# GpSimd computes the pool branch's moving sums ahead of two weight splits, and their consumers move up by two or three steps

## The reference

```python
h = rms_norm(x, g_mix_norm[l])
z = h @ w_in[l]
q_lat, kv_lat, k_rope = z[..., :o1], z[..., o1:o2], z[..., o2:o3]
uv, pin = z[..., o3:o4], z[..., o4:]
a = mla_mixer(...)                       # 4 heads, causal softmax over 512 tokens
gm = sgu_mixer(uv, ...)                  # gate branch
po = pool_mixer(pin, w_pool[l], pool_scale[l])
mix = concatenate([rms_norm(a), rms_norm(gm), rms_norm(po)])
x = x + mix @ w_out[l]

def pool_mixer(p, w_pool, pool_scale):
    for g, win in enumerate((2, 4, 8, 16)):
        # mean over the last `win` tokens, minus the token itself
        outs.append((cs - cs_shift) / count - xg)
    y = einsum('bsgc,gcd->bsgd', m, w_pool)
    return y * pool_scale
```

## Time and profile before

| what | value |
|---|---|
| median of 3 runs | 2698.09 us (2691.52 to 2700.82) |
| profiled execution | 2697.78 us, span 2695.9 us |
| mean granted TensorE clock | 0.985 of full speed |
| PE busy | 2607.8 us, 97% of the span |
| DVE busy | 1173.2 us, 44% |
| ACT busy | 501.1 us, 19% |
| POOL busy | 1626.1 us, 60% |

### The profile page before, as it was taken

One profiled execution on the slowest core, in us unless ns is written; L12 is line 12 of the kernel. 1 busy time (PEld: TensorE's weight loads), 2 busy tenths in 40 slices (PEclk: granted clock), 3 DMA queues, 4 the chain that ended last, 5 costly groups with the idle time before them and its releaser, 6 DMA issues.

```text
span 2695.9 us, 31577 instructions
## 1 busy us (share of the span) xinstructions
PE 2607.8 (97%) x11906; PEld 2142.7 (79%) x11906; DVE 1173.2 (44%) x1678; ACT 501.1 (19%) x849; POOL 1626.1 (60%) x1113
## 2 busy tenths in 40 slices
PE   7889999999899999999999999999999999999997
PEld 6768888888578888887888888888788878888885
DVE  5754443036644440345540513783467155504325
ACT  3342111023421110201200103200310044100022
POOL 5526667664266676666676766676246615767763
PEclk9999999999899999999999999999999999999998
DMA  4102222231022222222232223222112202222221
GB/s 153 63 16 94 97 105 94 93 115 63 16 94 98 104 93 94 94 94 94 102 106 97 93 94 104 93 98 104 48 47 100 103 32 73 94 106 94 94 93 63
DMA packets 36892, 236.71 MB, mean 88 GB/s; under 512 B 4048, under 2 KB 5584, under 8 KB 9168
## 3 DMA queue, kind: packets, MB, share of 16 engines
q1 hardware_dynamic: 33456, 230.78, 24.6%
q10 hardware_dynamic: 3360, 4.85, 0.6%
HBM read 233.51 MB, written 2.10 MB: 87 GB/s over the span
## 4 chain that ended last, share of the span: by engine, by line
PE 93%; DVE 4%; ACT 1%; issue 1%; POOL 0%; DMA 0%; DVEq 0%; SPq 0%; POOLq 0%; ACTq 0%
PE psum L469 29%; PE psum L470 28%; PE psum L471 28%; PE psum L918 2%; PE psum L902 1%; PE psum L680 1%; PE psum L927 1%; PE psum L790 1%; PE psum L806 0%; DVE work L1335 0%; PE psum L499 0%; DMA x_res<-in_x 0%; POOL w_low L411 0%; PE psum L752 0%; DVE stat L1676 0%
## 5 line engine op out<-in xcount | busy, mean ns | idle before, releaser
L411 POOL TENSOR_TENSOR w_low<-w_stage,w_high 128x512 fp32r<-128x512 f32 x864 | 1178.7, 1395 | 18.0
L407 POOL TENSOR_SCALAR w_high<-w_stage 128x2048 fp32r<-128x2048 f32 x216 | 416.3, 1928 | 1014.8 <-PE psum L471 1003.5
L469 PE MATMUL psum<-x_high,w_high 128*128 128x512 f32 x1664 | 654.2, 393 | 17.0 <-DVE x_low L1351 17.0
L470 PE MATMUL psum<-x_low,w_high 128*128 128x512 f32 x1664 | 649.3, 390 | 0.0
L471 PE MATMUL psum<-x_high,w_low 128*128 128x512 f32 x1664 | 649.0, 390 | 0.0
L469 PEld LDWEIGHTS psum<-x_high,w_high 128*128 128x128 f32 x1664 | 313.4, 188 | 85.1 <-issue 17.1
L470 PEld LDWEIGHTS psum<-x_low,w_high 128*128 128x128 f32 x1664 | 313.3, 188 | 67.0 <-issue 2.2
L471 PEld LDWEIGHTS psum<-x_high,w_low 128*128 128x128 f32 x1664 | 313.3, 188 | 65.2
L469 PE MATMUL psum<-mlp_high,w_high 128*128 (+1 forms) x576 | 224.3, 389 | 2.8 <-DVE mlp_low L1468 2.8
L1392 DVE TENSOR_TENSOR psum<-psum,x_res 128x512 f32<-128x512 f32 x56 | 39.2, 700 | 426.8 <-PE psum L471 423.8
L471 PE MATMUL psum<-mlp_high,w_low 128*128 (+1 forms) x576 | 224.2, 389 | 0.0
(11 more groups left out here) (266 smaller groups left out, 3486.2 us busy)
## 6 DMA issues: line engine op xcount, KB each, us to landing
w_stage<-in_wstream SPq DMA_DIRECT2D x216, 1024.0 KB, 4.9
x_res<-in_x SPq DMA_DIRECT2D x2, 1024.0 KB, 11.7
out_x<-attn_out SPq DMA_DIRECT2D x8, 256.0 KB, 2.1
inv_count_sb<-in_inv_count ACTq DMA_DIRECT2D x2, 512.0 KB, 9.0
ple_proj<-in_p ACTq DMA_DIRECT2D x2, 512.0 KB, 3.7
qk<-in_mask ACTq DMA_DIRECT2D x1, 576.0 KB, 3.8
w_spat<-in_spatial ACTq DMA_DIRECT2D x2, 256.0 KB, 5.5
diag_sb<-in_diag ACTq DMA_DIRECT2D x2, 256.0 KB, 9.7
```

The lines of the kernel that those rows point to most:

```text
L407: pool.tensor_scalar(wh[:, s, :], stage[:, s, :], 1.0, 1.0, ALU.mult, ALU.mult).then_inc(high_written, 1)
L411: last = pool.tensor_tensor(wl[:, s, part], stage[:, s, part], wh[:, s, part].bitcast(F32), ALU.subtract)
L469: pe.matmul(out, wa, ra, start=start, stop=False)
L470: pe.matmul(out, wa, rb, start=False, stop=False)
```

## The change

GpSimd does slabs 0 to 5, then the moving sums, then slabs 6, 7 and the rest. Before, it did slabs 0 to 7, then the moving sums, then the rest. On PE `pool_products` moves from step 11 to step 8, and the two `token_sum` jobs from steps 13 and 15 to steps 11 and 13. On ACT `pool_scaled` moves from step 12 to step 10. On DVE `pool_sum` moves from step 14 to step 12. No instruction is added or removed.

```diff
@@ gpsimd
-                    split_run(at, p.slab + 8)
-                    at = p.slab + 8
+                    split_run(at, p.slab + 6)
+                    at = p.slab + 6
                     pool.wait_ge(phase_landed, 16 * (FIRST_LOADS + MIX_LOADS * (p.layer + 1)))
                     windows(p)
@@ tensor
-... 5: gate_products, 11: pool_products,
-    13: lambda: token_sum(p, 2, 2), 15: lambda: token_sum(p, 3, 2)}
+... 5: gate_products, 8: pool_products,
+    11: lambda: token_sum(p, 2, 2), 13: lambda: token_sum(p, 3, 2)}
@@ scalar
-                between = {8: gate_squares, 12: pool_scaled}
+                between = {8: gate_squares, 10: pool_scaled}
@@ vector
-... 9: gate_sum, 14: pool_sum}
+... 9: gate_sum, 12: pool_sum}
```

More of the change, by code:

```diff
@@ L781, in pool_products @@
                         last.then_inc(z_done, 1)
-                between = {1: lambda: input_tile(2), 2: lambda: input_tile(3), 5: gate_products, 11: pool_products,
-                           13: lambda: token_sum(p, 2, 2), 15: lambda: token_sum(p, 3, 2)}
+                between = {1: lambda: input_tile(2), 2: lambda: input_tile(3), 5: gate_products, 8: pool_products,
+                           11: lambda: token_sum(p, 2, 2), 13: lambda: token_sum(p, 3, 2)}
                 def values(h):
@@ L1660, in low_out @@
                         tt(mix_low[k], tile, mix_high[k].bitcast(F32), ALU.subtract).then_inc(split_low, 1)
-                between = {2: lambda: pool_input(0), 3: lambda: pool_input(1), 6: lambda: gate(0), 7: lambda: gate(1), 9: gate_sum, 14: pool_sum}
+                between = {2: lambda: pool_input(0), 3: lambda: pool_input(1), 6: lambda: gate(0), 7: lambda: gate(1), 9: gate_sum, 12: pool_sum}
                 steps = HEADS * TOK
```

## The result

The changed kernel is slower by a little: 2702.25 us median (2698.34 to 2706.14, 20 runs) against 2697.64 us (2691.52 to 2703.84, 20 runs) before, a ratio of 1.0015 with a 95% interval of 1.0009 to 1.0021. That is 4.6 us, within the 0.3% that were forecast as "no change", inside the range of 2691 to 2706, a quarter of a microsecond above the forecast's own range of 2695 to 2702, and not the 0.4 us of the forecast.

The account below looks back on a forecast made before the run. PE and DVE waiting for each other in two 54 us stretches was taken as the bound. Terms of -1.7 + 1.6 + 0.3 gave +0.2 us per phase, +0.4 for two: median 2698.5 us, range 2691 to 2706.

Parts of the forecast that it names:

- the forecast's 141.6: GpSimd, first loop: the splits of slabs 6 and 7 end at about 141.6 us, at no cost to PE.
- What that does to DVE: DVE, steps 6 to 8: instructions wait for GpSimd's splits, making divisions late and costing PE 1.6 us per phase, bounds 0 to 2.9.
- a case at full clock: PE at step 8: at full clock it loses 0.9 us to the division of step 8, ending at 141.6 us.
- one at half clock: PE at `values(1)`: if it runs at half clock as before, step 7's whole 2.3 us of lateness pass through.
- Moving sums earlier: GpSimd: sums start as each tile is ready, from 110.1 us, ending about 126.6; nothing waits for their start.
- The terms behind it: Behind step 8's transposes: pool scaling, token sums and `pool_sum` gain 1.7 us per phase; ACT behind a late DVE costs 0.3.
- Moving the second sum to step 13: PE, step 13: the second token sum costs 0.91 us there, after a 0.6 us wait for `pool_sum`.
- the 0.3 for ACT: ACT, step 10: pool scaling stands behind late exponential and copy, so PE's token sum may wait; 0.3 us per phase.
- the slower rival: Steps 7 to 10: GpSimd's lock beside DVE's critical instructions costs 2.9 us, pool gain lost; 2703 to 2707 us, chance 0.18.
- The move does nothing at step 8: PE, step 8: bank 3 is freed late, so the products merely change place; 1.86 us per phase return, 2702 us; chance 0.05.
- the faster rival: PE, `values(1)` at full clock: DVE's later divisions stay inside PE's own time; some 2693 us in total, chance 0.25.

Follow-up runs that it names:

- e1: The kernel before with only GpSimd's new order (sums, then slabs 6 and 7), jobs of PE, ACT and DVE at their old steps: 2705.86 us, ratio 1.0020 to before.
- e3: The changed kernel with GpSimd waiting, after the sums, for a count reached with step 10's scores before splitting slabs 6 and 7: 2699.78 us, ratio 1.0000 to before.
- e6: The changed kernel with slabs 6 and 7 each split in 8 + 8 short GpSimd instructions instead of 1 + 4: 2695.95 us, ratio 0.9986 to before.
- e2: The changed kernel with slab 6 split ahead of the moving sums and only slab 7 behind them: 2695.42 us, ratio 0.9991 to before.

## Why the prediction was partly right

**What held.** The bound: PE and DVE waiting for each other in two short stretches, and DVE waiting for the end of GpSimd's running instruction. The moving sums started at once. PE did not wait for the late splits themselves. The products went into PE's wait at step 8, and L1685 still ended it. The first token sum stands right behind the scores of step 11. GpSimd's end came at 27.96 us after the scores of step 3, where the forecast's 141.6 is 27.5. Each loop changed by less than 2 us. The total stayed within 0.3%.

**The step that failed: "What that does to DVE".** Its term was 1.6 us a loop, the middle of a case at full clock (0.9) and one at half clock (2.3). It measured 2.94 and 3.02 us, beyond the upper bound of 2.9. Walked from POOL's rows, the division of step 7 was to end 2.3 us late. It ended 135.21 - 111.53 = 23.68 us after the scores of step 3 against 21.08 before, 2.6 us late, and `values(1)`, over its 2.42 us at full clock in both, took 0.34 us more (3.65 against 3.31). The two make 2.94. Of the 1.34 us that the term was short, 0.7 are the choice: nothing in the rows spoke for full clock at `values(1)`. PE had waited for DVE there before, and was to wait again. The case of 2.3 should have been taken, not a mean of two cases, one of which had no row for it.

The walk's 2.3 itself came near by luck, as two errors in it cancel. "Moving sums earlier" was put at no cost, as nothing waits for the start of the sums. But DVE's steps 3 to 5 met them, and the maximum of step 6, where the walk began, was 0.7 us late already (10.23 us after the scores of step 3 against 9.52). From there to the division of step 7 DVE lost 1.9 us, less than the walk's 2.3. In the second loop the parts are others. The division of step 7 ended 3.8 us late (23.46 against 19.70): 1.6 us at the maximum of step 6, half of it the gate products' clock (2.82 us and not 1.97), and 2.2 behind it. `values(1)` gave 0.7 us back, as it took 3.68 us and not 4.39. So its 3.02 is near the first loop's 2.94 by chance. The division of step 8 ended 28.04 us after the scores of step 3, 3.4 us late and not 2.9, but PE reached it another 1.5 us later.

**The terms behind it** came out right in their sum. Forecast -1.7 and +0.3, that is -1.4 us from step 8's transposes to the end of the loop. Measured: 46.62 to 44.67 and 45.72 to 44.64 us, -1.95 and -1.08, a mean of -1.5. That the mean fits is in part luck, as the clock moved both loops: `values(2)` took 4.11 us before and 3.29 after in the first loop, 2.88 and 3.32 in the second. Up to step 11's transposes, where no `values` stands, the gain was 1.2 us in both loops, where 1.3 less the 0.3 for ACT was forecast. ACT's 0.3 did not come: the first token sum starts 0.1 us behind the scores of step 11. Step 11's transposes were to be within 1 us of before and were 1.75 us late, which is the failed term again. Moving the second sum to step 13 was counted at 0.91 us and a wait of 0.6. The wait was 0.96.

**The rivals.** With 2.9 us in the profiles' loops and 4.6 us in the medians, the outcome lies nearer to the slower rival, which began at 5.2 us, than to the forecast of 0.4. That rival had the right mechanism (e1, e3, e6), a place that e1 shows, and a price at step 8 that was right (2.9). It missed that the gain behind step 8 stays, and its sum of 2 x (2.9 - 0.3) doesn't follow from its terms: with the gain gone they give 2 x 2.9 = 5.8 us and more, and no row shows the 0.3. "The move does nothing at step 8" is refuted by the trace. Of the faster rival, no sign: `values(1)` took 3.65 and 3.68 us, not 2.42, and PE ran at 0.81 of its clock in both loops after the change. (The "up to 3" of that rival is 8.21 x (1 - 0.53) = 3.9 by its own row.)

```profile
111.50:165.50 54.00, 39.20 (x171) 24.31 (x169) 41.47 (x91) 26.38 (x62) 26.22 (x20) 0.81 0.11 39
664.60:718.60 54.00, 39.25 (x171) 24.37 (x169) 41.40 (x91) 26.51 (x62) 26.25 (x20) 0.81 0.11 39
```

GpSimd is busy 26.2 us of the 54 where it was 22.4 and 22.7, and DVE's busy time, which holds its waits for GpSimd, grew by 2.4 and 1.8 us. The added split is 7.7 us of GpSimd's time. GpSimd's column grows by less, as the first tile's sums now run largely ahead of the stretch.

**What stays open.** The medians moved by 4.6 us (2.4 to 5.7 by the interval) and the two loops in the profiles by 2.9. The 2.9 is inside the interval, and the rest can't be told from what the clock does from one profile to the next. e1's loops moved by 9.1 us and its median by 6.7 (2.4 to 8.6), the same kind of gap the other way.

## What to carry to other kernels

Moving work on GpSimd is not free because GpSimd is idle enough: ask which DVE instructions run beside it at the old and at the new place, and keep GpSimd's work beside stretches where DVE is off the path, as e2 does with slab 6. Where that can't be had, cut GpSimd's instructions short, since DVE waits for one instruction at a time, not for the job. Start a walk ahead of the first job that moves, not at the first one that looks critical. When two of a walk's cases differ by the clock, take the one in which the engine has just been waiting.

## What the runs showed of the hardware

A DVE instruction over 128x1 took 0.16 us with GpSimd idle, and in the examples above 1.52 us behind a 1.9 us GpSimd instruction and 0.36 us behind one over 128x256. This agrees with the exclusive lock of the Trainium skill, SBUF — State Buffer, section "Who interferes with whom". The same split of two slabs took GpSimd 15.6 us in 1 + 4 instructions each and 20.0 us in 8 + 8, both beside a busy DVE. And outside the changed stretches the same code took 46.9 to 51.6 us from one profile to the next, in five kernels that are the same up to there, a spread as large as the effect that was measured.
